# Two-layer encoder kernel: 512-column query and key projections, interleaved head transposes and a reordered last mixer head

## The reference

```python
# layer 0 mixer (mLSTM, 8 heads, both directions)
q, k, v, o, gates = split(rmsnorm(x) @ w_in)          # q, k: 64 wide per head; v, o: 128
Sqk = (q @ k.T) * exp(D - m)                          # D from cumulated gates, masked
num = Sqk @ v + (state part);  h = num / max(|den|, exp(-m))
hs = (h_fwd + h_bwd);  hs = hs * rsqrt(mean(hs*hs)) * head_g * sigmoid(o)
x = x + hs @ w_out
# layer 1 mixer (differential attention, 8 heads of two halves)
q, k, v = split(rmsnorm(x) @ w_qkv);  q, k = rope(rmsnorm(q)), rope(rmsnorm(k))
a = softmax(q1 @ k1.T) - lam * softmax(q2 @ k2.T);  o = rmsnorm(a @ v) * (1 - lambda_init)
x = x + o @ w_out
# PEER, in both layers
q = rmsnorm(x) @ w_query                              # 16 blocks of 128 columns
s = q_block @ sub_keys_block;  top 16 of each, top 16 of the pairs, gates = softmax
x = x + sum over the chosen experts of gate * gelu(h . u_e) * v_e   # 16384 experts, 16 per head
```

## Time and profile before

| | us |
|---|---|
| median of 3 runs | 1901.79 (1900.55 to 1902.08) |
| profiled execution | 1901.35 |
| its span, first to last instruction | 1899.6 |
| q and k units of layer 0 | about 19 to 42.7 |
| layer 0 head loop | about 70.8 to 123 |
| query units and scores, layer 0 / layer 1 | 157.5 to 211.7 / 1098.5 to 1152.6 |
| dense PEER part, layer 0 | 211.7 to 953 |
| q, k, v projections of layer 1 | 961 to 1027.7 |
| attention loop of layer 1 | 1033.3 to 1068.5 |

### The profile page before, as it was taken

One profiled execution on the slowest core, in us unless ns is written; L12 is line 12 of the kernel. 1 busy time (PEld: TensorE's weight loads), 2 busy tenths in 40 slices (PEclk: granted clock), 3 DMA queues, 4 the chain that ended last, 5 costly groups with the idle time before them and its releaser, 6 DMA issues.

```text
span 1899.6 us, 33581 instructions
## 1 busy us (share of the span) xinstructions
PE 1865.7 (98%) x11578; PEld 1577.8 (83%) x11578; DVE 1422.9 (75%) x2610; ACT 972.8 (51%) x1379; POOL 105.9 (6%) x71
## 2 busy tenths in 40 slices
PE   8999999999999999999999999999999999999998
PEld 7768988888888888888876698888888888888887
DVE  5565588988888888655578756889888888886555
ACT  5464555655554444444465645556555544444444
POOL 0000343000000000000000003420000000000000
PEclk9999999999999999999999999999999999999999
DMA  6325455555555555555544244555555555555554
GB/s 226 122 89 166 151 193 187 177 178 177 172 171 168 176 176 176 189 190 196 193 173 143 78 156 156 187 189 184 173 172 170 171 172 177 177 177 189 198 190 164
DMA packets 89488, 326.17 MB, mean 172 GB/s; under 512 B 10064, under 2 KB 10192, under 8 KB 89040
## 3 DMA queue, kind: packets, MB, share of 16 engines
q1 hardware_dynamic: 88848, 323.00, 52.0%
q10 hardware_dynamic: 576, 2.33, 0.3%
HBM read 324.24 MB, written 1.05 MB: 171 GB/s over the span
## 4 chain that ended last, share of the span: by engine, by line
PE 91%; DVE 6%; ACT 2%; issue 1%; DMA 0%; DVEq 0%; ACTq 0%
PE ps L1464 21%; PE ps L1715 12%; PE ps L1717 12%; PE ps L1716 12%; PE ps L1462 12%; PE ps L1663 3%; PE ps L1461 3%; PE ps L1449 2%; PE ps L1450 2%; PE ps L1451 2%; DVE wl L814 2%; PE ps L1485 2%; PE ps L1487 2%; PE ps L1486 2%; PE ps L1644 1%
## 5 line engine op out<-in xcount | busy, mean ns | idle before, releaser
L814 DVE TENSOR_TENSOR wl<-raw,wh 128x1024 fp32r<-128x1024 f32 x572 | 700.5, 1228 | 192.5 <-ACT wh L463 183.9
L463 ACT ACTIVATE wh<-raw 128x1024 fp32r<-128x1024 f32 x612 | 645.0, 1056 | 349.5 <-PE ps L1717 171.2
L1464 PE MATMUL ps<-hT,wh 128*128 128x512 f32 x1792 | 637.6, 395 | 0.0
L1462 PE MATMUL ps<-hT,wl 128*128 128x256 f32 x2048 | 529.1, 279 | 0.0
L1462 PEld LDWEIGHTS ps<-hT,wl 128*128 128x128 f32 x2048 | 385.9, 188 | 20.9
L1715 PE MATMUL ps<-wh,hT 128*128 128x512 f32 x1024 | 401.8, 392 | 0.4 <-DVE big L798 0.4
L1717 PE MATMUL ps<-wh,hT 128*128 128x512 f32 x1024 | 398.9, 390 | 0.0
L1716 PE MATMUL ps<-wl,hT 128*128 128x512 f32 x1024 | 398.3, 389 | 0.0
L1464 PEld LDWEIGHTS ps<-hT,wh 128*128 128x128 f32 x1792 | 336.1, 188 | 68.5
L1717 PEld LDWEIGHTS ps<-wh,hT 128*128 128x128 f32 x1024 | 192.2, 188 | 40.6
L1715 PEld LDWEIGHTS ps<-wh,hT 128*128 128x128 f32 x1024 | 192.3, 188 | 39.7 <-issue 1.0
(11 more groups left out here) (223 smaller groups left out, 1775.3 us busy)
## 6 DMA issues: line engine op xcount, KB each, us to landing
raw<-stream SPq DMA_DIRECT2D x612, 512.0 KB, 3.4
big<-keys ACTq DMA_DIRECT2D x2, 1024.0 KB, 7.8
x<-x_in SPq DMA_DIRECT2D x1, 1024.0 KB, 5.4
out<-x SPq DMA_DIRECT2D x4, 256.0 KB, 2.2
sm<-small ACTq DMA_DIRECT2D x1, 228.5 KB, 5.6
pos_i<-positions ACTq DMA_DIRECT2D x1, 1.0 KB, 6.5
```

Source lines behind the costliest of these rows:

```text
L463: act.activation(wh[:, r, :], raw[:, r, :], ACT.Copy).then_inc(high_ready, 1)
L814: dve.tensor_tensor(wl[:, r, :], raw[:, r, :], wh[:, r, :].bitcast(F32), ALU.subtract).then_inc(made_low(unit), 1)
L1462: pe.matmul(near, w_l[:, kd, :], hTh[:, kd, :], start=False, stop=False)
L1464: i = pe.matmul(wide, w_h[:, kd, :], both, start=False, stop=(kd == KD - 1))
```

## The change

1. The qk and the wq units use `up_both_halves`. ACT copies the second half of the bank to SBUF, and DVE adds the first half to it (`qk_add`; one add per wq unit). The scores of a token half wait for four units at a time (`wq_out`), no longer for all sixteen.
2. `ml_decay` writes each direction in two pieces of 256 columns, each followed by its mask matmul.
3. `ml_tanh(2)` stands ahead of the fifth head's exponentials in ACT's program. In the eighth head's iteration the norm of the first four heads, their transposes and splits stand ahead of that head's weighted values; `ml_tanh(3)` moves with them.
4. The 32 transposes of layer 1's q and k are cut into four parts of 8, ahead of units (3,0), (4,0), (5,0) and (5,2) of the projections; ACT makes all the copies.
5. At the end of the attention loop the first two head transposes come one place earlier; one small DVE operation per step changes its form.

```diff
+        QKT_BEFORE = (3, 0), (4, 0), (5, 0), (5, 2)
@@ scalar: qk units
-                act.activation(qkT[:, u, :], ps[:, 4 + u % 3, 0:S], ACT.Copy,
-                               scale=ML_SCALE if u < 4 else 1.0).then_inc(qk_out, 1)
+                act.activation(qkT[:, u, :], ps[:, 4 + u % 3, S:2 * S], ACT.Copy,
+                               scale=ML_SCALE if u < 4 else 1.0).then_inc(qk_half, 1)
@@ scalar: head loop
             for h in range(HEADS + 2):
-                if h < HEADS:
-                    ml_exp(h)
-                    ahead(unit_of["vo"] + U_VO // 2 + h)
-                if 1 <= h <= HEADS:
-                    ml_forward(h - 1)
                 if h == HEADS // 2:
                     ml_tanh(2)
                 if h == HEADS - 1:
                     preload(ACT.Sqrt)
                     head_std(0, 0)
-                    preload(ACT.Exp, 1)
-                if h == HEADS:
+                if h < HEADS:
+                    ml_exp(h)
+                if h < HEADS - 1:
+                    ahead(unit_of["vo"] + U_VO // 2 + h)
+                if 1 <= h <= HEADS:
+                    ml_forward(h - 1)
+                if h == HEADS - 1:
+                    ahead(unit_of["vo"] + U_VO - 1)
                     for pair in range(2):
                         heads_transposed(1, pair, gain(4))
                     ml_tanh(3)
+                if h == HEADS:
                     ahead(unit_of["wo0"])
@@ scalar: wq units
-                    if u % 2 == 0:
-                        act.wait_ge(used, unit + 1)
-                        act.activation(qT[:, u, :], ps[:, 4 + u % 4, 0:S], ACT.Copy).then_inc(wq_out_a, 1)
+                    act.wait_ge(used, unit + 1)
+                    act.activation(qT[:, u, :], ps[:, 4 + u % 4, S:2 * S], ACT.Copy).then_inc(wq_half, 1)
@@ scalar: q, k, v of layer 1
+            def qkt_got(part):
+                for b in (2 * (part % 2), 2 * (part % 2) + 1):
+                    act.wait_ge(qkt_mm, 2 * part + b % 2 + 1)
+                    ...
+                    act.activation(qkT_da[:, q:q + 2, :]..., ps[:, b, :], ACT.Copy).then_inc(qkt_out, 1)
             for nb in range(6):
+                if nb in (3, 4):
+                    qkt_got(nb - 3)
                 tokens_made(act, ahead, qkv_mm, "qkv", nb, 1)
...
+                    if nb == 4:
+                        qkt_got(2)
+                        ahead(unit_of["qkv"] + 4 * nb + 6)
+                        qkt_got(3)
@@ vector: head loop
+                if h == HEADS - 1:
+                    head_scale(0, 0)
+                    for pair in range(2):
+                        head_norm(hg, pair)
                 ml_weights(h)
...
-            head_scale(0, 0)
-            for pair in range(2):
-                head_norm(hg, pair)
-            ml_den(HEADS - 1)
-            heads_transposed(1, 0, gain(4))
+            for pair in range(2):
+                heads_transposed(1, pair, gain(4))
+            ml_den(HEADS - 1)
+            ahead(unit_of["vo"] + U_VO - 1)
             ml_output(HEADS - 1)
-            heads_transposed(1, 1, gain(4))
@@ vector: wq units
-                    if u % 2 == 1:
-                        dve.wait_ge(used, unit + 1)
-                        dve.tensor_copy(qT[:, u, :], ps[:, 4 + u % 4, 0:S]).then_inc(wq_out_v, 1)
+                    dve.wait_ge(wq_half, U_WQ * l + u + 1)
+                    dve.tensor_tensor(qT[:, u, :], ps[:, 4 + u % 4, 0:S], qT[:, u, :], ALU.add).then_inc(wq_out, 1)
@@ tensor
-            by_columns(unit_of["qk"], U_QK, lambda u: 4 + u % 3, qk_bank)
+            for u in range(U_QK):
+                qk_bank(u)
+                up_both_halves(4 + u % 3, unit_of["qk"] + u)
@@ tensor: ml_decay
-                    pe.matmul(ps[:, b, :]..., pick[0:64, c:c + 1].to_broadcast([64, P]),
-                              rowM[0:64, :].unsqueeze(1).to_broadcast([64, NT, S]), start=True, stop=False)
                     for s in range(NT):
                         at_ = s * S + s * P
-                        i = pe.matmul(ps[:, b, at_:at_ + P], ident_b[:], m[:], start=False, stop=(s == NT - 1))
+                        pe.matmul(ps[:, b, s * S:(s + 1) * S], pick[0:64, c:c + 1].to_broadcast([64, P]), rowM[0:64, :],
+                                  start=True, stop=False)
+                        i = pe.matmul(ps[:, b, at_:at_ + P], ident_b[:], m[:], start=False, stop=True)
@@ tensor: head loop
+                if h == HEADS - 1:
+                    pe.wait_ge(e_ready, HEADS)
+                    for pair in range(2):
+                        head_transposes(1, pair)
                 ml_values(h)
-            for pair in range(2):
-                head_transposes(1, pair)
@@ tensor: wq units and scores
-                by_columns(unit_of[f"wq{l}"], U_WQ, lambda u: 4 + u % 4, wq_bank)
-                pe.wait_ge(wq_out_a, U_WQ // 2 * (l + 1))
-                pe.wait_ge(wq_out_v, U_WQ // 2 * (l + 1))
+                for u in range(U_WQ):
+                    wq_bank(u)
+                    up_both_halves(4 + u % 4, unit_of[f"wq{l}"] + u)
                 for t in range(NT):
                     for b in range(4):
+                        pe.wait_ge(wq_out, U_WQ * l + 4 * b + 4)
@@ tensor: layer 1
+            def qkt(part):
+                pe.wait_ge(qkn_ready, part + 1)
+                if part >= 2:
+                    pe.wait_ge(qkt_out, 2 * part - 2)
+                ...
-            pe.wait_ge(qkn_ready, 4)
-            for b in range(8):
-                ...
+            for nb in range(6):
+                for q in range(4):
+                    if (nb, q) in QKT_BEFORE:
+                        qkt(QKT_BEFORE.index((nb, q)))
+                    token_unit(...)
@@ attention loop: scalar n in (17, 18), vector n in (18, 19), tensor head_transposes ahead of da_values
```

More of the change, by code:

```diff
@@ L267, in program @@
         wo_mm = sem("wo_mm")
-        wq_out_a = sem("wq_out_a")
-        wq_out_v = sem("wq_out_v")
+        wq_half = sem("wq_half")
+        wq_out = sem("wq_out")
+        qk_half = sem("qk_half")
         score_mm = sem("score_mm")
@@ L592, in _ @@
                 if h == HEADS:
-                    preload(ACT.Sqrt)
+                    preload(ACT.Sqrt, 1)
             head_std(1, 0)
@@ L708, in _ @@
             act.activation(lam[:, 2:4], lam[:, 0:2], ACT.Exp).then_inc(lam_ready, 1)
+            def qkt_got(part):
+                for b in (2 * (part % 2), 2 * (part % 2) + 1):
+                    act.wait_ge(qkt_mm, 2 * part + b % 2 + 1)
+                    q = 4 * part + 2 * (b % 2)
+                    act.activation(qkT_da[:, q:q + 2, :].rearrange("p a t -> p (a t)"), ps[:, b, :], ACT.Copy
+                                   ).then_inc(qkt_out, 1)
             for nb in range(6):
+                if nb in (3, 4):
+                    qkt_got(nb - 3)
                 tokens_made(act, ahead, qkv_mm, "qkv", nb, 1)
@@ L728, in _ @@
                 ahead(unit_of["qkv"] + 4 * nb + 5)
[L730 to L733, removed]
             def da_exp(n):
@@ L886, in _, with qk_add @@
             ahead(unit_of["qk"])
+            def qk_add(u):
+                dve.wait_ge(qk_half, u + 1)
+                dve.scalar_tensor_tensor(out=qkT[:, u, :], in0=ps[:, 4 + u % 3, 0:S],
+                                         scalar=ML_SCALE if u < 4 else 1.0, in1=qkT[:, u, :],
+                                         op0=ALU.mult, op1=ALU.add).then_inc(qk_out, 1)
             dve.wait_ge(gate_mm, 1)
@@ L895, in _ @@
             i.then_inc(fabs_ready, 1)
+            qk_add(0)
             dve.tensor_copy(lgate[:, :, 0, 0:8], g4[:, :, 0, 0, :])
             dve.tensor_copy(lgate[:, :, 1, 8:16], g4[:, :, 1, 0, :])
+            ahead(unit_of["qk"] + 1)
+            qk_add(1)
             dve.wait_ge(softplus_ready, 1)
@@ L903, in _ @@
             i.then_inc(lgate_ready, 1)
-            ahead(unit_of["qk"] + U_QK - 1)
+            for u in range(2, U_QK):
+                ahead(unit_of["qk"] + u)
+                if u < U_QK - 1:
+                    qk_add(u)
             dve.wait_ge(rows_mm, 1)
@@ L1333, in _ @@
             ahead(unit_of["qkv"] + U_QKV - 1)
-            for b in range(1, 8, 2):
-                dve.wait_ge(qkt_mm, b + 1)
-                dve.tensor_copy(qkT_da[:, 2 * b:2 * b + 2, :].rearrange("p a t -> p (a t)"), ps[:, b, :]
-                                ).then_inc(qkt_out_v, 1)
             def da_max(n):
@@ L1348, in da_sums @@
                 chain(dve.reciprocal(zz[:, n, 2:3], zz[:, n, 1:2]))
-                dve.tensor_scalar(zz[:, n, 3:4], zz[:, n, 2:3], lam[:, 5:6], zz[:, n, 0:1], ALU.mult, ALU.mult
-                                  ).then_inc(rz_ready, 1)
+                dve.scalar_tensor_tensor(out=zz[:, n, 3:4], in0=zz[:, n, 2:3], scalar=lam[:, 5:6], in1=zz[:, n, 0:1],
+                                         op0=ALU.mult, op1=ALU.mult).then_inc(rz_ready, 1)
             def da_difference(n):
@@ L1383, in _ @@
                     da_got(n - 5)
```

(14 more changed lines are left out.)

34 lines of the change are left out of this document (17 added, 17 removed).

## The result

| | us |
|---|---|
| changed kernel, median of 5 runs | 1890.8 (1889.36 to 1892.11) |
| kernel before, median of 5 runs beside it | 1901.2 (1899.65 to 1902.08) |
| ratio | 0.9944, 95% interval 0.9932 to 0.9956 |
| profiled execution, before / after | 1901.35 / 1889.36 |

The kernel is faster by 10.4 us. Forecast were a gain of 8.7 and a time of 1893.0. The profiled executions differ by 12.0.

The account below looks back on a forecast made before the run. PE, busy for 98% of the span, was taken as the bound. Terms 4.2 - 4.8 + 2.0 + 2.7 + 1.7 + 1.9 + 1.0 = 8.7 us gained gave 1893.0 us, range 1885.5 to 1897.5.

Parts of the forecast that it names:

- Wide units: qk and query units: 512-column form saves 0.08 us per unit, and idle before the scores goes; 4.2 us gained.
- Decay: Decay exponents: two pieces per direction add passages in and out of the 64-row form; 4.8 us lost.
- The reading that the pieces would be free by this: Decay, rival: the split costs nothing or gains; 1888.2 us, or 1885.0 with 3.2 gained; chance 17%.
- The fifth head's tanh: Fifth head: tanh ahead of the exponentials removes PE's wait; 2.0 us gained, bounds 1.5 and 2.0.
- The last head: Last head: transposes before values remove waits, 2.7 us gained; the clock fall behind goes too, 1.7 us gained.
- The fear for the next two pairs' transposes: Output projection: transposes of the other two pairs, about 8 us in, named as the next danger; no size given.
- Layer 1's transposes: Layer 1's q and k transposes among the projections: waits mostly go; 1.9 us gained, bounds 0.5 and 2.4.
- The loop's end: Attention loop's end: earlier transposes remove PE's wait for the first head split; 1.0 us gained, bounds 0 and 1.05.
- waits only move: Reordered places, rival: early operations delay later ones; 5.5 us less, 1898.5, or half, 1895.8; 21% shared, worst end 6%.
- The slower case, falls brought by the alternation: Decay, rival: alternating 64 and 128 rows brings clock falls of 1.7 us each; 1903 to 1907 us; chance 4%.

Follow-up runs that it names:

- e1: Changed kernel with the decay put back to one 512-column matmul per direction; 1886.09 us, ratio 0.9920 to the kernel before.
- p1: Changed kernel with the decay's operands given 128 rows instead of 64, still two pieces per direction; 1883.37 us, ratio 0.9904 to the kernel before.
- e2: Kernel before with only the wide qk and wq units and the scores waiting for four units; 1897.26 us, ratio 0.9971.
- e4: Kernel before with only layer 1's transposes moved among the projections and the attention loop's end reordered; 1898.66 us, ratio 0.9984.
- p4: Kernel before with nine unread bf16 products filling the 2.3 us wait ahead of the output projection at the last head; 1899.53 us, ratio 0.9993.
- r2: Kernel before, unchanged, run and profiled a second time; 1902.54 us, ratio 0.9999.
- e3: Kernel before with only the earlier fifth-head tanh and the reordered last head; 1893.51 us, ratio 0.9959.
- p2: Changed kernel with the decay's operands given 128 rows and one 512-column matmul per direction; 1880.91 us, ratio 0.9896 to the kernel before.
- p3: Changed kernel with a direction's two 64-row decay pieces side by side, before both masks; 1885.04 us, ratio 0.9914 to the kernel before.
- r1: Changed kernel, unchanged, run and profiled a second time; 1891.89 us, ratio 0.9949 to the kernel before.

## Why the prediction was right, and where its sizes were off

- **Wide units.** Mechanism and size hold: 0.08 per unit at qk (0.54 for seven), 4.1 for the two sets of query units with their scores where I had 3.6. The Trainium skill's isolated gap of N/2.4 + 2.5 ns ("TensorE: Matmul & The Clock Gate", "Back-to-back issue gap") would have given an estimate of a quarter of that, 0.02; the trace measured 0.08 again.
- **Decay.** 4.8 forecast, 4.80 measured by e1. p1 shows that the number of rows is the cause: with 128 the 0.2 is gone. The Trainium skill says that weight loads are pulled ahead of running matmuls when the row groups don't conflict or when they target the background weight buffer ("TensorE: Matmul & The Clock Gate", "Step-by-step: what each phase is for"). The reading that the pieces would be free by this does not agree with the traces: the load was pulled ahead with 128 rows (74.80) and not with 64 among 128 (0.35 of idle ahead of it). Whether such a change of rows counts as a conflict in that sentence, no run here can tell.
- **The fifth head's tanh.** This is the term that was mis-sized. I had 2.0 for the wait, and 2.0 as its upper bound too; it measured 2.27, and behind the wait a fall of the clock went too, 1.6. In the one profile that I had, PEclk behind that wait was 1.00, and an equal fall stood at 72.7 to 76.1. I counted neither. In the four other traces that keep the wait (e2, e4, p4, r2) the fall stands behind it; in the seven that lack it (the changed kernel twice, e1, e3, p1, p2, p3) the head loop has no fall at all, also not at 73, though the wait of 1.33 ahead of 70.82 is there in all twelve. So that fall was worth having in the sum whichever of the two places it takes. That it goes with this wait is read from these counts; no run fills this wait alone, as p4 does the other.
- **The last head.** 2.7 and 1.7 forecast, 2.76 and 1.6 measured; p4 shows the link between the idle and the clock. The fear for the next two pairs' transposes did not come true.
- **Layer 1's transposes.** 1.9 forecast, 2.08 measured, with one wait of 0.73 left.
- **The loop's end.** 1.0 forecast; 1.26 to 1.29 where no clock fall stands in the stretch (r1, e1, e4, p1, p2, p3), 0.3 in the first profile, where one does.
- **Why the waits were worth more than their brackets.** A bracket counts from the end of the last matmul, and that matmul's length overlaps the next one when there is no wait. At the fifth head the values begin at 97.53 and the unit behind them at 101.16, 3.63 later; without the wait it is 1.36 later (94.51 and 95.87 in e3). The difference is 2.27, the bracket 2.03. The loop's end gives the same 0.2: 1.26 to 1.29 for a bracket of 1.05. For each of the two sets of query units 15 x 0.08 and the bracket of 0.56 are 1.8, and 2.0 went. So the sum was low by 0.2 for each of these waits.

Added up with the falls that the kernel itself decides: 0.6 + 4.1 - 4.8 + 2.3 + 1.6 + 2.8 + 1.6 + 2.1 + 1.3 = 11.6. The medians of e2, e3 and e4 and the 4.7 of part 2 give 4.7 + 8.4 + 3.3 - 4.7 = 11.7. With part 2 taken from the medians beside each other, 5.4, the second sum is 11.0. The measured 10.4 lies within what the executions vary by: its interval is 8.4 to 12.9. r1 gave 10.4 once more, so the 0.6 to 1.3 between the sums and the measurement may be real; no run tells what they would be. By the stages the forecast's 8.7 was low by about 3, half of it the uncounted fall, the rest five terms of 0.1 to 0.5 in one direction; by the time it was low by 1.7. That the time came nearer than the stages is luck in part. The twelve us between the two profiled executions hold 1.45 of a half clock that stands later at the start, which is the execution's: r1 has gate transposes at 21.99, r2 at 22.11.

Of the rivals, "waits only move" had a small part: a wait of 0.39 at the last head and one of 0.73 ahead of the attention. The slower case, falls brought by the alternation, is refuted: eight alternations per head and PEclk 1.00 from 70 to 120 in the changed kernel.

What stays open: what lets the fall come behind one wait in one execution and behind another in the next, and why it comes at the attention loop's end in three of twelve traces (changed kernel, e3, p4). Also a stretch of 1.1 to 1.2 that the dense part of either layer takes longer in some traces (layer 0 in e2, p4, r1 and r2, layer 1 in e1, e4, p1, p3 and r2), at full clock and without a wait. In r2, laid beside the first profile of the same kernel, it grows evenly by 0.15 per 25 us between about 400 and 595 us, and not before or behind. No experiment was made on these.

## What to carry to other kernels

On PE, a matmul group whose stationary operand has 64 rows paid about 0.2 us for going in and out among 128-row work, whether it was one matmul of 256 columns, one of 512, two of 256 or, in the scores, eight of 256; fill the operand up with zero rows where rows cost nothing, or put such matmuls side by side, and never interleave them with others one by one. A wait of PE that went was worth its bracket and 0.2 more at the fifth head, at the loop's end and ahead of the scores. Of the nine waits of 2.0 to 2.3 us that the twelve traces have in layer 0's head loop and at its end, eight had a half clock behind them that cost 1.6 more. Where one profile shows a clock fall at one place, look for every wait that could have had it, and count falls by a second profile.

## What the runs showed of the hardware that was not expected

- With 128 rows throughout, one 512-column float32 matmul and two bf16 masks take 0.33 us from the start of one direction to that of the next, less than the 0.44 that the sum of their paces in other places gave; the two masks cost 0.09 together there (p2).
- Every fall of the clock inside the kernels lasted 3.4 us. In and behind layer 0's head loop, where PE was busy, it cost 1.6; at the attention loop's end, where PE waits in between, it cost 0.96 in the changed kernel, 0.86 in e3 and 0.65 in p4.
- Where the half clock at the start lies is the execution's. In four traces (the changed kernel, e2, e3, e4) it is over by 14.4 us, ahead of the gate unit's start at 14.5 to 14.6, and the gate's transposes stand at 20.5 to 20.6. In seven it stands between 15.2 and 19.4, in the gate unit, and in the first profile of the kernel before from 11.3 to 18.1; the gate's transposes stand at 21.8 to 22.1 in these eight. With the two stretches of 1.1 to 1.2 in the dense parts this adds up to an estimate of 3.8 us, beside the 1.4 to 5.3 us by which runs of one kernel differ; only one execution of each run has a trace, so the link is not shown.
